# Conditioning pieces, weight splits, sums, picks and output of a two-layer fused trunk put in another order

## The reference, cut to what matters

```
layer 0: x += gate * even_mixer(rms(x)*(1+scale)+shift)   # 8-head attention || short conv, then w_o
         x += gate * swiglu(...)                          # d_ff 2816
layer 1: x += gate * (conv31(glu(h@pw1+b)) -> layernorm -> silu -> @pw2 + b_pw2)
         x += gate * moe(...)                             # router, top 2 of 8 experts, d_ff 3584
```

## Time and profile before

| | us |
|---|---|
| median of 3 runs | 1640.77 |
| the profiled execution | 1641.62 |
| its span | 1639.8 |
| TensorE busy in the span | 1532.2 (93%) |
| VectorE busy | 1193.7 (73%) |
| ScalarE busy | 980.2 (60%) |
| mean granted TensorE clock | 0.959 |

### The profile page before, as it was taken

One profiled execution on the slowest core, in us unless ns is written; L12 is line 12 of the kernel. 1 busy time (PEld: TensorE's weight loads), 2 busy tenths in 40 slices (PEclk: granted clock), 3 DMA queues, 4 the chain that ended last, 5 costly groups with the idle time before them and its releaser, 6 DMA issues.

```text
span 1639.8 us, 23483 instructions
## 1 busy us (share of the span) xinstructions
PE 1532.2 (93%) x8464; PEld 1294.2 (79%) x8464; DVE 1193.7 (73%) x1185; ACT 980.2 (60%) x988; POOL 15.4 (1%) x20
## 2 busy tenths in 40 slices
PE   4876999999899879999999999999999999999995
PEld 2854989999875778887888888888888888888884
DVE  1544454444785657887988988988988988988885
ACT  1433453343445436776777777777777777777772
POOL 0010000000000000000000000000000000000000
PEclk9888989999899788998999999999999999999998
DMA  8657347665468126998999999999999999999992
GB/s 331 254 218 254 126 159 238 235 200 181 155 219 287 53 77 223 365 366 274 363 373 324 365 372 328 367 370 324 367 368 331 367 367 334 367 365 333 354 367 115
DMA packets 319027, 468.86 MB, mean 286 GB/s; under 512 B 11473, under 2 KB 271713, under 8 KB 312818
## 3 DMA queue, kind: packets, MB, share of 16 engines
q1 hardware_dynamic: 317744, 464.83, 82.6%
q10 hardware_dynamic: 866, 2.03, 0.3%
q0 software_dynamic: 352, 1.13, 0.2%
HBM read 466.81 MB, written 1.13 MB: 285 GB/s over the span
## 4 chain that ended last, share of the span: by engine, by line
PE 83%; DMA 5%; DVE 5%; issue 4%; ACT 2%; SPq 0%; POOL 0%; ACTq 0%; DVEq 0%; POOLq 0%
PE bank L1442 17%; PE bank L1444 17%; PE bank L1443 17%; PE bank L1448 5%; PE bank L1449 5%; PE bank L1450 5%; DMA raw<-moe_gu 3%; PE bank L1759 2%; PE bank L1870 2%; PE bank L1459 2%; PE bank L1898 1%; PE bank L1716 1%; PE bank L1717 1%; PE bank L1474 1%; PE bank L1718 1%
## 5 line engine op out<-in xcount | busy, mean ns | idle before, releaser
L1357 DVE TENSOR_TENSOR low<-raw,high 128x2048 fp32r<-128x2048 f32 x333 | 757.6, 2290 | 127.5 <-ACT high L761 120.0
L761 ACT ACTIVATE high<-raw 128x2048 fp32r<-128x2048 f32 x333 | 635.8, 1919 | 187.0 <-DMA raw<-moe_gu 117.1
L1442 PE MATMUL bank<-high,hidH 128*128 128x512 f32 x896 | 351.4, 392 | 0.7 <-issue 0.7
L1444 PE MATMUL bank<-high,hidL 128*128 128x512 f32 x896 | 350.2, 391 | 0.0
L1443 PE MATMUL bank<-low,hidH 128*128 128x512 f32 x896 | 349.6, 390 | 0.0
L1448 PE MATMUL bank<-hidH,high 128*128 128x256 f32 x736 | 216.8, 295 | 29.5 <-DVE hidL L882 12.2
L1449 PE MATMUL bank<-hidL,high 128*128 128x256 f32 x736 | 214.0, 291 | 0.0
L1450 PE MATMUL bank<-hidH,low 128*128 128x256 f32 x736 | 213.8, 291 | 0.0
L1442 PEld LDWEIGHTS bank<-high,hidH 128*128 128x128 f32 x896 | 168.9, 188 | 35.5 <-issue 0.9
L1444 PEld LDWEIGHTS bank<-high,hidL 128*128 128x128 f32 x896 | 168.8, 188 | 35.4
L1443 PEld LDWEIGHTS bank<-low,hidH 128*128 128x128 f32 x896 | 169.0, 189 | 34.7
(11 more groups left out here) (218 smaller groups left out, 1363.0 us busy)
## 6 DMA issues: line engine op xcount, KB each, us to landing
raw<-moe_gu SPq DMA_DIRECT2D x448, 512.0 KB, 5.4
raw<-moe_down SPq DMA_DIRECT2D x112, 1024.0 KB, 6.5
raw<-ada_w SPq DMA_DIRECT2D x48, 1024.0 KB, 5.2
raw<-ffn_gu SPq DMA_DIRECT2D x44, 512.0 KB, 4.9
raw<-ffn_down SPq DMA_DIRECT2D x11, 1024.0 KB, 7.2
raw<-w_in SPq DMA_DIRECT2D x8, 1024.0 KB, 8.6
raw<-conv_pw SPq DMA_DIRECT2D x16, 512.0 KB, 4.3
raw<-w_o SPq DMA_DIRECT2D x4, 1024.0 KB, 13.2
```

Source lines behind the costliest of these rows:

```text
L761: a.activation(high[:, m % SPLITS, :], raw[:, n % RAWS, :], ACT.Copy).then_inc(S("high_ready"), 1)
L1357: v.tensor_tensor(low[:, n % RAWS, :], raw[:, n % RAWS, :], high[:, m % SPLITS, :].bitcast(F32), ALU.subtract).then_inc(S("low_ready"), 1)
L1442: pe.matmul(out, xh, wh, start=start, stop=False)
L1444: return pe.matmul(out, xl, wh, start=False, stop=stop)
```

## The change

The ring's order, and with it the orders of the engines, are changed in these places. (1) Four pieces of the first conditioning group are used before and between the sums of the first norm; `win 0 0` moves ahead of pieces 5 to 7. (2) `win 1 0` and `win 1 1` move ahead of group 2 in the ring, and their `low` parts stand before and between the two maxima; three pieces of group 2 move behind w_o's; the transposed probabilities go to banks 4 and 5, so they no longer wait for group 2. (3) Sums of the second norm stand within w_o's last piece, and pieces of groups 2 and 3 in its waits; `ffn b 0` is split later. (4) Five pieces of group 4 stand in the third norm's waits, three behind the units of pw1, six of group 5 within the convolution and two behind the layer norm's sums. (5) The layer norm's sums are made in two parts; pw2's bias leaves TensorE and is added to `xT` on GpSimd (two instructions, the second over 128x2048). (6) Picks are made before the gate values. (7) In the last expert VectorE adds the earlier experts' part in units 7 to 10 (four instructions of 128x1024), and the output is written in four parts, before SyncE reads the flag that decides on a second pass.

```diff
+    ada(0, 0, 5)
+    order.append(("win", 0, 0))
+    ada(0, 5, 8)
+    order.extend([("win", 0, 1), ("win", 2, 0), ("win", 2, 1)])
     ada(1, 0, 3)
...
-    order.extend([("win", 3, 0), ("win", 3, 1)])
-    ada(2, 0, 8)
-    order.extend([("win", 1, 0), ("win", 1, 1)])
-    order.extend([("wo", 0, 1), ("wo", 1, 1), ("wo", 0, 0), ("wo", 1, 0)])
-    for u in range(FFN_UNITS):
-        order.extend([("ffn", "a", u), ("ffn", "b", u)])
-        if u == 0:
-            ada(3, 0, 2)
-        else:
-            order.append(("ffn", "d", u - 1))
-            if u <= 6:
-                ada(3, u + 1, u + 2)
+    order.extend([("win", 3, 0), ("win", 3, 1), ("win", 1, 0), ("win", 1, 1)])
+    ada(2, 0, 5)
+    order.extend([("wo", 0, 1), ("wo", 1, 1), ("wo", 0, 0), ("wo", 1, 0), ("ffn", "a", 0)])
+    ada(2, 5, 8)
+    order.append(("ffn", "b", 0))
+    ada(3, 0, 2)
+    for u in range(1, FFN_UNITS):
+        order.extend([("ffn", "a", u), ("ffn", "b", u), ("ffn", "d", u - 1)])
+        if u <= 6:
+            ada(3, u + 1, u + 2)
     order.append(("ffn", "d", FFN_UNITS - 1))
-    order.extend([("pw1", k, u) for u in range(4) for k in "ab"])
-    ada(4, 0, 8)
-    ada(5, 0, 8)
-    order.extend([("pw2", h, kh) for h in (0, 1) for kh in (0, 1)])
+    ada(4, 0, 3)
+    order.extend([("pw1", "a", 0), ("pw1", "b", 0)])
+    ada(4, 3, 5)
...
+            def write_out(passes):
+
+                for i, (h, tt) in enumerate([(h, tt) for h in range(2) for tt in range(TILES)]):
+                    cols = slice(h * 512, (h + 1) * 512)
+                    sp.wait_ge(S("y_ready"), 4 * passes + i + 1)
+                    sp.dma_start(outs[tt][0][:, cols], xrow[:, tt, cols]).then_inc(S("y_out"), 16)
+                sp.wait_ge(S("y_out"), 64 * (passes + 1))
+
+            write_out(0)
...
+            b0 = COLS["pw2_b"][0]
+            pool.wait_ge(S("ada_out"), 10)
+            st.do(pool.tensor_tensor(pw2_gb[:, :, :], mod[:, 1, 2], par[:, b0:b0 + KT].unsqueeze(2).to_broadcast(
+                [P, KT, 2]), ALU.mult), "pw2_bias")
+            pool.wait_ge(S("residual"), 8)
+            st.mark(pool.tensor_tensor(
+                xT[:, :, :].rearrange("p k (t n) -> p (k t) n", t=TILES),
+                xT[:, :, :].rearrange("p k (t n) -> p (k t) n", t=TILES),
+                cat(pw2_gb[:, :, :]).unsqueeze(2).to_broadcast([P, KT * TILES, P]), ALU.add), "x_biased")
...
-            named("wo", 0, 1)
...
+                st.mark(a.activation(cat(probT[:, g % 2]), bank[:, 4 + g % 2, :], ACT.Copy), "probT_ready")
...
             probabilities_out(1)
+            named("wo", 0, 1)
             product(a, "win", 1, 1)
...
-                probabilities_out(g)
+            probabilities_out(2)
+            probabilities_out(3)
             a.wait_ge(S("sc_gated"), 1)
             st.mark(a.activation(hidH[:, 4:8, :], hid[:, 4:8, :], ACT.Copy), "sc_high")
+            probabilities_out(4)
+            probabilities_out(5)
+            named("wo", 1, 1)
             for tt in range(TILES):
                 a.wait_ge(S("pv_group"), 2 if tt == 0 else 6)
                 st.mark(a.activation(hidH[:, 0:4, tt * P:(tt + 1) * P],
                                      bank[:, 2 + tt, :].rearrange("p (c n) -> p c n", c=4), ACT.Copy), "at_high")
...
-            named("ffn", "b", 0)
             for p in range(4):
                 square_pair(1, p)
+            named("ffn", "b", 0)
             modulate_split(1, {})
...
                     conv_out(k - 1)
+                    named("pw2", 0, k - DVE_TILES - 1)
             conv_out(KT - 1)
-            named("pw2", 0, 0)
-            named("pw2", 0, 1)
-            named("pw2", 1, 0)
...
+            named("pw2", 1, 0)
...
                 picked(0)
+                if not passes:
+                    a.wait_ge(S("x_T"), 2)
+                    st.mark(a.activation(xrow[:, 1, :], cat(bank[:, 4:6, :]), ACT.Copy), "x_row")
...
                 scaled(0, p)
+            named("win", 0, 0)
             rows_out(0)
             mod_out(0)
             gain_scale(0)
-            named("win", 0, 0)
...
+            named("win", 1, 0)
             scores_max(0, cat(bank[:, 0:2, :]))
+            named("win", 1, 1)
             scores_max(1, cat(bank[:, 2:6, :]))
-            named("win", 1, 0)
             normalise(0, prob_c, P)
-            named("win", 1, 1)
             v.wait_ge(S("v_ready"), 2)
...
             normalise(1, prob_l, 2 * P)
-            rows_out(2)
-            mod_out(2)
             named("wo", 0, 1)
...
                     "sc_low")
+            named("wo", 1, 1)
             for tt in range(TILES):
                 v.wait_ge(S("at_high"), tt + 1)
...
-            named("wo", 1, 1)
             named("wo", 0, 0)
             named("wo", 1, 0)
             named("ffn", "a", 0)
-            named("ffn", "b", 0)
+            residual(0)
+            rows_out(2)
+            norm_sums_read(1)
+            mod_out(2)
             gain_scale(1)
-            residual(0)
-            norm_scale(1, 8)
-            modulate_split(1, {})
+            spread(NORM_C, TILES, 8)
+            modulate_split(1, {0: ("ffn", "b", 0)})
...
-            conv_taps(rest, 11, 24)
-            rows_out(5)
-            conv_taps(rest, 24, 27)
-            mod_out(5)
-            conv_taps(rest, 27, TAPS)
+            conv_taps(rest, 11, 25)
             named("pw2", 0, 0)
+            conv_taps(rest, 25, TAPS)
             named("pw2", 0, 1)
...
-            named("pw2", 1, 0)
             v.wait_ge(S("ln_ssum"), 1)
             root_mean(tile_sums(4, 0), D)
+            rows_out(5)
...
+            mod_out(5)
+            named("pw2", 1, 0)
             gate_out(0)
...
+            v.wait_ge(S("x_biased"), 1)
             residual(2)
...
             first_expert("b", 0)
-            first_expert("a", 1)
...
             first_of_max(LG2, 10, 12, MASK2)
+            st.do(v.tensor_tensor(r(M), r(MASK1), r(MASK2), ALU.add), "chosen")
             st.do(v.tensor_tensor(small[:, 0:2], small[:, 10:12], small[:, 8:10], ALU.subtract), "top2_diff")
-            st.do(v.tensor_tensor(r(M), r(MASK1), r(MASK2), ALU.add), "chosen")
...
-            st.do(v.tensor_reduce(small[:, 14:15], bank[:, 6, 16:16 + EXPERTS], AX, ALU.max), "route_part")
-            st.do(v.tensor_copy(flag[0:1, 0:1], small[0:1, 14:15]), "flag_ready")
+            st.do(v.tensor_reduce(small[:, 14:15], bank[:, 6, 16:16 + EXPERTS], AX, ALU.max), "slots_read")
...
+                        if last and 7 <= u <= 10:
+                            earlier_experts(passes, u - 7)
...
+                    for h in range(2):
+                        for tt in range(TILES):
...
+                            if last:
+                                v.scalar_tensor_tensor(ys, bank[:, 4 + h + 2 * tt, :], gcol[:, 2 + tt:3 + tt], gate[:, tt, cols],
+                                                       ALU.mult, ALU.mult).then_inc(S("y_part"), 1)
+                                v.wait_ge(S("y_part"), e * 4 + (4 * ge + i + 2))
+                                v.tensor_tensor(xs, xs, ys, ALU.add).then_inc(S("y_ready"), 1)
...
+                def earlier_experts(passes, step):
+
+                    tt = step // 2
+                    if step % 2 == 0:
...
+                        st.do(v.tensor_tensor(xhat[:, tt, :], xhat[:, tt, :], gate[:, tt, :], ALU.mult), "y_gated")
+                    else:
+                        st.do(v.tensor_tensor(xrow[:, tt, :], xrow[:, tt, :], xhat[:, tt, :], ALU.add), "y_gated")
...
                 else:
                     tokens_low()
+                    first_expert("a", 1)
+                    gate_values()
                     parts(0, 3, LEAD)
...
-            v.wait_ge(S("x_row"), TILES)
-            for tt in range(TILES):
-                st.do(v.tensor_tensor(xhat[:, tt, :], xhat[:, tt, :], gate[:, tt, :], ALU.mult), "y_gated")
-                st.do(v.tensor_tensor(xrow[:, tt, :], xrow[:, tt, :], xhat[:, tt, :], ALU.add),
-                      "y_ready" if tt == 1 else "y_gated")
...
 
+            pe.wait_ge(S("cond_ready"), 1)
+            ada_piece(0, 0)
+            ada_piece(0, 1)
             pe.wait_ge(S("const_in"), 16)
-            for p in range(4):
-                norm_sum(0, p)
+            norm_sum(0, 0)
+            norm_sum(0, 1)
+            ada_piece(0, 2)
+            norm_sum(0, 2)
+            norm_sum(0, 3)
+            ada_piece(0, 3)
             broadcast(bank[:, 7, TOK:2 * TOK], TILES, 2)
-            pe.wait_ge(S("cond_ready"), 1)
-            for k in range(KT):
+            for k in range(4, KT):
                 ada_piece(0, k)
...
-            for k in range(KT):
+            for k in range(5):
                 ada_piece(2, k)
             pe.wait_ge(S("exp_c"), HEADS)
             chunk(("win", 1, 0), 0, pairs_of(0), None, False, {}, 0)
-            ada_sum(2)
...
                 if g == 0:
-                    pe.wait_ge(S("ada_out"), 6)
+                    pe.wait_ge(S("exp_l"), HEADS)
```

(50 more changed lines are left out.)

115 lines of the change are left out of this document (59 added, 56 removed).

## The result

The changed kernel takes 1594.16 us (median; 1591.72 to 1595.92) against 1640.69 us of the kernel before on the same chip: a ratio of 0.9713, 95% interval 0.9693 to 0.9733, faster. The forecast was 1598 in a range of 1583 to 1617. The profiled execution took 1595.92 us, its span is 1594.1. First the page of the changed kernel: its span, its busy times, and TensorE's clock in 40 slices, which is lowest from 558 to 598 us, in the last norm, the routing and the gather.

What follows compares the result with a forecast made beforehand. The prediction took TensorE's order as the bound: experts at full clock for 997 us, a dense part with holes and low clock. Terms summed to 43.8 us off 1641.6, giving 1598, range 1583 to 1617.

Steps and rivals of the forecast that it cites:

- Start: Up to the first weight product: it comes at 35.4 instead of 43.46 us, a gain of 8.
- Attention: Attention to w_o's end: waits for `win 1 0` and group 2 go, pieces run at full clock; gain 21.3 us.
- the rival with a starved ring: Attention and later norms: pieces arrive late, group 2's piece 5 before `wo 0 0`; 8 to 18 us, 1606 to 1616; chance 0.17.
- First SwiGLU unit: Between `b0` and `a1`: TensorE stands 11 us for late loads, splits and SiLU; loss 9.8 us including low clock.
- The rival without the hole: First SwiGLU unit: pieces come as fast as TensorE wants or the clock holds; 1586 us; chance 0.13.
- Third norm, pw1: Third norm to the convolution's start: added pieces and later splits delay products, full clock gives back 2; loss 3.6 us.
- Convolution to pw2: Convolution to the last norm: gains of 17.3 in taps and 3.7 in layer norm, loss 2.2 in pw2; together 18.8.
- The rival that put the point at 0.042 us an element: GpSimd's bias addition: 321 us at its power's price per element, layer norm waits, 1877 us; decides from 0.042; chance 0.04.
- Routing: Routing before the gather: picks need only the slots, ready at 610.0 instead of 615.65; gain 5.7 us.
- That stretch keeps its length: Experts: 997 us with TensorE busy in 991.6 at full clock; nothing changes but the last few us.
- End: After the last expert product: output in four pairs, then the flag read, ending at 1635.3 against 1639.4; gain 3 us.
- No gain by order alone: Whole kernel: the experts' stream is the true bound, later loads pay back an earlier start; 1632 to 1641; chance 0.05.

Runs made afterwards that it cites:

- e6: Changed kernel with the start undone: all eight group 0 conditioning pieces behind the norm's sums again, `win 0 0` behind them; 0.9760 of the kernel before.
- e2: Changed kernel, ring order only: last three group 2 pieces loaded ahead of `a0`, group 3's pieces 0 and 1 after unit 0's down piece; 0.9678 of the kernel before.
- e1: Changed kernel with unit 0's SiLU ahead of the splits of `b1` and `d0` on ScalarE, loads untouched; 0.9682 of the kernel before.
- e4: Changed kernel with the attention part about group 2 undone: all eight conditioning pieces and their sum around `win 1 0` again; 1604.24 us, 0.9764 of the kernel before.
- e5: Changed kernel with e2's ring order, and SyncE reading the flag before it writes the output; 0.9691 of the kernel before.
- e7: Changed kernel with GpSimd's addition of the pw2 bias made five times in a row instead of once; 1614.27 us in one run.
- e10: Changed kernel with the routing part undone: gate values ahead of the slots again, expert 0's third low part ahead of the logits; 0.9774 of the kernel before.
- e3: Changed kernel with the first gate rows and their bias addition back ahead of the first pw2 piece; 0.9734 of the kernel before.
- e8: Changed kernel with a norm sum moved behind the last down piece, and group 5's piece 7 moved into a layer norm wait; 0.9743 of the kernel before.

## Why the prediction was right, point by point

The time is right to 1.9 us in 45.7, and part of that is luck: the misses in the table are 16.5 us without their signs. The largest is the experts' stretch, which was put at nothing. One term was added up wrongly: the parts given for the third norm and pw1, 1.9 + 1.4 + 3.2 - 2, make 4.5 and not 3.6, so that the sum should have read 42.9 and the time 1599. (The second norm's end, 179.7 + 9.6, is 189.3 and not 189.7, which changes no term.)

**Start.** Right in kind, 1.7 us too much. Piece 7 is used at 31.69 after a wait for its transfer of 0.89, one us later than forecast, and the norm's modulation took 0.7 more. e6 shows that the gain is kept to the end.

**Attention.** `win 1 0` starts right behind the five pieces, the wait for the sum of group 2 is gone, and both pieces run at full clock (gains of 1.75 and 2.0 us where the terms were 2.0 and 1.9). Piece 5 of group 2 is used at 160.86 without a wait, so the rival with a starved ring did not come. The 2 us that are missing are the products with values: the forecast was a gain of 1.1, measured is a loss of 0.4. ScalarE splits `wo 0 1`, which lands at 141.0, ahead of two copies of probabilities, and TensorE waits 0.97 and 1.22 us for them (0.22 and 1.22 in the second profile). The prediction had not put the new place of this split in any term. About 0.5 is lost before the scores end.

**First SwiGLU unit.** Right: 7.3 plus 2.1 us of low clock against 9.8. e2 shows that the ring slot is the cause, e1 that the order of splits more than doubles it, e4 that most of it comes with the attention part (3.36 us stay). The rival without the hole (1586) was wrong as a forecast of this kernel, and it is about what e2 and e5 reach (1589.67 and 1590.97, or 1588 and 1590 by their ratios on this chip).

**Third norm, pw1.** 3.2 against 3.6 in the first profile; in the second the norm took 6.3 us more by the clock alone. The 3.6 was no better known than that.

**Convolution to pw2.** The tap stage is right to 1 us. In the layer norm and in pw2 two sizes are off by 2.2 us each and cancel: the norm lost more than I counted, since the gate rows left it, and the first pw2 piece took 8.65 us at a clock of 0.65, where the sum had 5.8. The prediction had charged it for the gate rows only, not for the clock.

**GpSimd.** The addition took 3.71 us, near VectorE's end of the bounds (2.3) and far from the power's price (321). It held up the taps by 3.4 us, and TensorE would have waited had they been the bound: VectorE's taps end at 507.3, two us before the sums start. e7 shows that what is left of the cover is 2 us, not 42: the limit is the held-up taps, not GpSimd's queue. Without the addition's 3.4 us the taps would have ended 5.4 us before the sums, where the prediction had 1.7. By that 1.7 its sentence on both pages, that taps 4.5 us later leave the sum as it is, does not follow: 2.8 us would have been lost. That nothing was lost is the spare time it had not counted. The rival that put the point at 0.042 us an element named the wrong place.

**Routing.** 4.3 against 5.7. The wait ahead of the gather went from 6.76 to 1.21 us, 5.6 of the 5.7. The router's products and transposes ahead of it took 1.2 us more, at a lower clock, in no term of the sum. Windows of the kernel before, then of the changed one:

```profile
596.65:609.48 12.83, 12.56 (x72) 12.09 (x72) 9.98 (x26) 7.31 (x10) 0.00 (x0) 0.65 0.00 0
```

```profile
563.25:577.29 14.04, 13.94 (x74) 13.61 (x74) 9.23 (x31) 8.83 (x12) 0.00 (x0) 0.59 0.00 1
```

**Experts.** "That stretch keeps its length" is the step that failed. Over the eleven profiles of kernels with the new routing order it is 990.1 to 997.9 us, 993.9 in the mean; in the two of the kernel before 996.95 and 1002.84. The length goes by the clock. From the beginning of TensorE's wait at the end of expert 0 to its first scatter, windows of the changed kernel and then of the kernel before:

```profile
701.46:717.07 15.61, 14.87 (x82) 12.90 (x83) 11.97 (x12) 12.04 (x12) 0.00 (x0) 1.00 0.91 299
```

```profile
739.28:761.48 22.20, 19.62 (x83) 17.26 (x83) 14.25 (x12) 13.62 (x14) 0.00 (x0) 0.77 0.66 219
```

The same work takes 6.6 us more with the wait of 2.58 and the fall behind it. The chain that ends the wait is the same in both: ScalarE waits for a gate or up piece to land, splits it (from 697.57 and 737.23), and VectorE's product that TensorE needs begins 4.16 us later; but the split starts 3.9 us before TensorE is through with its products in the changed kernel, and 2.1 before. So in this pair it is a transfer that lands later against TensorE's work.

In this pair of profiles 3.8 of the 46 us come from this stretch, by the means 6.0. Whether the change brings them is open. For it: at this place the wait was 0.72 to 1.44 us in the eleven, and longer in all three profiles with the old order around the routing, 2.58 and 1.86 in the kernel before and 1.69 in e10. Against it: in e10 no fall followed there, its stretch of 997.89 us is no longer than e3's 997.93 with the new order, and the 8.5 to 10 us that it cost cannot be told, by the intervals, from the 5.4 of the picks. Why the order should matter to transfers a hundred us later was not tried.

**End.** 4.2 us against 3. The four pairs took 5.6 us as forecast. The units of the last expert took 8.41, as in the kernel before: the 1 us charged for the four long instructions in them was not paid.

**No gain by order alone** (1632 to 1641) is refuted by the result, and by e4, e6 and e10 in part: each loses in its own stage about what its part was said to bring.

## What to carry to other kernels

In a ring, ask of every piece that is moved which slot the pieces behind it now take: seven places on, a load waits for a use that used to be long past. Of the versions tried, the changed ring of e2 is the best find, at 0.9678, 0.9691 and 0.9695 in three kernels against 0.9713 and 0.9722 of the changed kernel: some 5 us, seen in the trace each time as 7 us in one stage, though the intervals touch. e1, which moves only splits, has 0.9682 and is no worse within them; the two together were not tried. Where a kernel alternates between full and half clock, compare stages over several profiles before a difference of 3 to 6 us is explained.

## What the runs showed of the hardware that was not expected

TensorE's clock fell or held at the same place in the same program. The fourteen profiles hold 98 ends of experts, each a wait, a gather and 48 products, 14.6 us behind the wait at full clock. Of the 68 with a wait under 0.89 us the clock fell behind none; of 26 with 0.89 to 1.70 us behind nine; of the four with 1.86 to 2.85 us behind all four. A fall cost 3.2 us (17.8 instead of 14.6) up to a wait of 1.57 us and 4.8 (19.4) from 1.63 on. In the third norm of e8 it fell with no wait ahead of it, in a row of sums and conditioning pieces; what makes it fall there no run shows. And a GpSimd addition in SBUF beside VectorE's two-input taps takes nine tenths of its length from them (3.35 of 3.73 us).
